# Expert weights in two more slots used once, the residual added in the last pass, selection in two halves

## The reference

```python
x = layer_norm(DN_ALPHA * x + mix, ln1_g[l], ln1_b[l])
ffn = expert_choice_ffn(x, w_router[l], w_gate_up[l], w_down[l])
x = layer_norm(DN_ALPHA * x + ffn, ln2_g[l], ln2_b[l])

def expert_choice_ffn(x, w_router, w_gate_up, w_down):
    aff = jax.nn.softmax(logits, axis=-1)             # 16 experts
    gate, idx = lax.top_k(jnp.swapaxes(aff, 1, 2), cap)   # cap = 64 tokens an expert
    h = jnp.einsum('becd,edf->becf', xs, w_gate_up)   # 1024 -> 2048
    ye = jnp.einsum('becf,efd->becd', jax.nn.silu(hg) * hu, w_down)
    ye = ye * gate[..., None]
    return jnp.zeros_like(x).at[bidx, idx].add(ye)
```

## Time and profile before

| | |
|---|---|
| median of 3 runs | 2457.54 us (2456.19 to 2457.84) |
| the profiled execution | 2456.17 us, its span 2454.4 us |
| TensorE busy / VectorE / ScalarE | 97% / 46% / 35% of the span |
| DMA | 401 MB, mean 163 GB/s |
| granted TensorE clock, mean | 0.990 of full |

### The profile page before, as it was taken

One profiled execution on the slowest core, in us unless ns is written; L12 is line 12 of the kernel. 1 busy time (PEld: TensorE's weight loads), 2 busy tenths in 40 slices (PEclk: granted clock), 3 DMA queues, 4 the chain that ended last, 5 costly groups with the idle time before them and its releaser, 6 DMA issues.

```text
span 2454.4 us, 31324 instructions
## 1 busy us (share of the span) xinstructions
PE 2373.1 (97%) x13306; PEld 1760.8 (72%) x13306; DVE 1137.8 (46%) x1595; ACT 869.1 (35%) x1403; POOL 124.3 (5%) x130
## 2 busy tenths in 40 slices
PE   8999999999999999999999999998999979999997
PEld 6788878888887888888888888865788733443332
DVE  6857676354543324354344463668433552131113
ACT  7554544243433323243233343347322411111111
POOL 0303021100000000000000001200000000000000
PEclk9999999999999999999999999999999989999998
DMA  5121313232224333242222332321322589999996
GB/s 168 70 73 67 104 54 111 70 121 87 102 86 155 120 108 136 79 158 79 93 103 103 112 138 103 115 105 48 127 96 78 200 346 416 429 427 430 428 429 260
DMA packets 117386, 400.97 MB, mean 163 GB/s; under 512 B 6656, under 2 KB 24704, under 8 KB 104320
## 3 DMA queue, kind: packets, MB, share of 16 engines
q1 hardware_dynamic: 113088, 384.29, 40.7%
q0 software_dynamic: 4160, 14.68, 1.7%
HBM read 385.06 MB, written 13.89 MB: 163 GB/s over the span
## 4 chain that ended last, share of the span: by engine, by line
PE 83%; DVE 7%; DMA 6%; ACT 3%; issue 1%; SPq 0%; POOL 0%; DVEq 0%; ACTq 0%; POOLq 0%
PE banks L94 20%; PE banks L96 19%; PE banks L95 19%; PE banks L2251 7%; PE banks L2289 5%; DMA activations_T<-w_gate_up_in 1%; DMA ring<-w_gate_up_in 1%; DMA work<-w_gate_up_in 1%; DVE ring_split L88 1%; DMA work<-o_b 1%; PE banks L1653 1%; DMA ring<-w_up_in 1%; PE banks L1665 1%; PE banks L2030 1%; PE banks L1683 1%
## 5 line engine op out<-in xcount | busy, mean ns | idle before, releaser
L94 PE MATMUL banks<-work_split,ring_split 128*128 128x512 f32 (+1 forms) x1560 | 617.4, 396 | 2.4 <-issue 0.8
L88 DVE TENSOR_TENSOR ring_split<-ring,halves_split 128x1024 fp32r<-128x1024 f32 x281 | 353.5, 1268 | 523.3 <-ACT halves_split L83 522.9
L95 PE MATMUL banks<-work_split,halves_split 128*128 128x512 f32 x1512 | 588.8, 389 | 0.0
L96 PE MATMUL banks<-activations_T_split,halves_split 128*128 128x512 f32 x1160 | 452.3, 390 | 0.0
L83 ACT ACTIVATE halves_split<-ring 128x1024 fp32r<-128x1024 f32 x281 | 293.7, 1055 | 310.9 <-PE banks L96 236.5
L94 PEld LDWEIGHTS banks<-work_split,ring_split 128*128 128x128 f32 x1560 | 293.0, 188 | 70.1 <-issue 8.1
L95 PEld LDWEIGHTS banks<-work_split,halves_split 128*128 128x128 f32 x1512 | 284.1, 188 | 55.7 <-issue 0.5
L96 PE MATMUL banks<-ring_split,work_split 128*128 128x512 f32 (+1 forms) x704 | 270.8, 385 | 0.0
L95 PE MATMUL banks<-halves_split,work_split 128*128 128x512 f32 x672 | 261.6, 389 | 0.0
L96 PEld LDWEIGHTS banks<-activations_T_split,halves_split 128*128 128x128 f32 x1160 | 217.7, 188 | 46.2
L2251 PE MATMUL banks<-work 128*64 128x512 f32 x464 | 150.7, 607 | 4.9 <-DMA work<-w_gate_up_in 2.6
(11 more groups left out here) (387 smaller groups left out, 3166.6 us busy)
## 6 DMA issues: line engine op xcount, KB each, us to landing
ring<-w_in_in SPq DMA_DIRECT2D x30, 2048.0 KB, 7.7
work<-w_gate_up_in SPq DMA_DIRECT2D x29, 2048.0 KB, 26.8
ring<-w_gate_up_in SPq DMA_DIRECT2D x21, 2048.0 KB, 26.2
ring<-w_down_in SPq DMA_DIRECT2D x19, 2048.0 KB, 9.2
work<-w_down_in SPq DMA_DIRECT2D x11, 2048.0 KB, 27.0
ring<-w_in_in SPq DMA_DIRECT2D x17, 1024.0 KB, 7.7
ring<-w_up_in SPq DMA_DIRECT2D x8, 2048.0 KB, 7.9
activations_T<-w_gate_up_in SPq DMA_DIRECT2D x8, 2048.0 KB, 26.9
```

Of the source, the lines that this page charges most:

```text
L88: s.mark(dve.tensor_tensor(R(dst), src, R(hi).bitcast(F32), ALU.subtract), what)
L94: pe.matmul(out, R(ll), R(rh), start=start, stop=False)
L95: pe.matmul(out, R(lh), R(rh), start=False, stop=False)
L96: return pe.matmul(out, R(lh), R(rl), start=False, stop=stop)
```

## The change

- **Slots.** `XH` (until it is filled with rows) takes load 0, and `acc` takes load 10; both are used once as slots. `slot_no` and `former` give the slot of a load and the load that was in it before; the other nine rotate over the rest. From load 20 on, load c again follows load c - 9.
- **Order of loads.** Loads 0 to 3 at first, 4 to 7 and 10 after `m31`, 8 after the logits, 9 after `x31`. Loads 11 to 19 come in halves, each half after half of the group that it follows. Load 11 follows load 1, 12 and 13 follow 2 and 3, and so on.
- **XH.** ScalarE writes `XH` block 0 only after group 0.0.
- **Residual.** `acc` is written by a copy in pass 0. In pass 6 VectorE re-adds high and low part in `XR` (`whole`), SP then broadcasts gain and bias into `XH`, between loads 90 and 91, and in pass 7 `keep` adds the residual to `acc`, a block at a time; `kept(n, t)` waits for block t.
- **Selection.** The 512 tokens of each expert stand as two rows of 256, on partitions 0 to 15 and 32 to 47. Both rows' 64 best are found together; the 64th best of the union is a threshold, and comparisons with it, summed over tokens by matmuls, give the places, equal values behind larger ones.

```diff
--- before.py
+++ after.py
...
-        lnrow = acc[:, 2:4, :]
...
+        posN = cols[:, 32:96].rearrange("p (t e) -> p t e", t=NT)
...
+        lnrow, kept_tmp = XH[:, 0:2, :], XH[:, 2:4, :]
...
-        eslot = [slot5, slot6, ring[2], ring[0], ring[1], ring[3], slot4, AT, slot8]
-        ES = len(eslot)
-        lnrow2 = eslot[(12 * NE // 2 - 8) % ES].rearrange("p k n -> p (k n)")[:, 0:2 * DM].rearrange("p (a b) -> p a b", a=2)
+        once = [x.rearrange("p t d -> p (t d)").rearrange("p (k n) -> p k n", k=KB) for x in (XH, acc)]
+        eslot = [slot5, slot6, ring[2], ring[0], ring[1], ring[3], slot4, AT, slot8] + once
+        ES = len(eslot) - 2
+
+        def slot_no(c):
+            return ES if c == 0 else ES + 1 if c == ES + 1 else (c - 1 if c <= ES else c - ES - 2) % ES
+
+        def former(c):
+            return c - ES - 1 if c <= 2 * ES + 1 else c - ES
+
+        lnrow2 = eslot[slot_no(12 * NE // 2 - 8)].rearrange("p k n -> p (k n)")[:, 0:2 * DM].rearrange("p (a b) -> p a b", a=2)
...
+            def flat(c):
+                return eslot[slot_no(c)].rearrange("p k n -> p (k n)")
+
             def load_half(sem, c, h, what):
...
+                part = slice(h * 2048, h * 2048 + 2048)
+                sem.mark(sp.dma_start(flat(c)[:, part], expert_rows(c // 12, c % 12)[:, part]), what)
+
+            def load(c):
+                e_w[slot_no(c)].mark(sp.dma_start(flat(c), expert_rows(c // 12, c % 12)), f"w{c}")
+
+            def freed(c):
+                return former(c) % 12 // 2, former(c) // 12
+
+            for c in range(4):
+                load(c)
+            sp.wait_ge(*l_pe("m31"))
+            for c in range(4, 8):
+                load(c)
+            load(ES + 1)
+            sp.wait_ge(*q_pe("logits"))
+            load(8)
+            sp.wait_ge(*l_act("x31"))
+            load(ES)
+            c = ES + 2
+            while former(c) < 10:
+                cs = [n for n in (c, c + 1) if freed(n) == freed(c)]
+                for h in range(2):
+                    sp.wait_ge(*e_pe(("half", "group")[h] + f"{freed(c)[0]}.0"))
+                    for n in cs:
+                        load_half(e_w[slot_no(n)], n, h, f"h{n}" if h == 0 else f"w{n}")
+                c += len(cs)
+            for c in range(c, LAST + 1):
+                n, p = freed(c if c < LAST else c + 1)
+                if (n, p) == (5, NE // 2 - 2) and freed(c - 1) != (n, p):
+                    sp.wait_ge(*e_vec("whole3"))
+                    for n, name in enumerate(("ln1_g_2", "ln1_b_2")):
+                        l_row.mark(sp.dma_start(lnrow[:, n, :], T[name].broadcast_to([P, DM])), name)
+                    n, p = freed(c)
+                sp.wait_ge(*e_pe(f"group{n}.{p}"))
+                if c < LAST:
+                    load(c)
                 else:
...
                     for h in range(2):
                         for e in range(2):
-                            load_half((e_h if h == 0 else e_w)[e if h == 0 else (c + e) % ES], c + e, h, f"{'hw'[h]}{c + e}")
+                            load_half((e_h if h == 0 else e_w)[e if h == 0 else slot_no(c + e)], c + e, h, f"{'hw'[h]}{c + e}")
...
-            for q in range(4):
+            first_T(0)
+            for q in range(1, 4):
                 first_T(q)
+                if q == 1:
+                    act.wait_ge(*e_pe("group0.0"))
+                    high(act, e_act, XH[:, 0, :], XR[:, 0, :], "XH0")
                 high(act, e_act, XH[:, q, :], XR[:, q, :], f"XH{q}")
...
             pe.wait_ge(*q_vec("aff"))
-            for t in range(NT):
-                mm = pe.transpose(psum[3][0:NE, t * P:(t + 1) * P], affN[:, t, :], ident)
+            for u in range(2):
+                mm = pe.transpose(psum[3][0:HB, u * P:(u + 1) * P], wide[:, u * HB:(u + 1) * HB], ident)
             q_pe.mark(mm, "affT")
-            pe.wait_ge(*q_vec("pos"))
-            for t in range(NT):
-                mm = pe.transpose(psum[2][:, t * NE:(t + 1) * NE], cum[0:NE, t * P:(t + 1) * P], ident[0:NE, 0:NE])
-            q_pe.mark(mm, "posN")
+            pe.wait_ge(*q_vec("thr"))
+            q_pe.mark(pe.transpose(psum[2][:, 0:NE], thr_row[0:NE, 0, :], ident[0:NE, 0:NE]), "thr")
+            pe.wait_ge(*q_vec("marks"))
+            pe.matmul(psum[1][:, 0:2 * NT * NE], m_incl, marks.rearrange("p a t e -> p (a t e)"), start=True, stop=False)
+            at = psum[1][:, 0:2 * NT * NE].rearrange("p (a t e) -> p a t e", a=2, t=NT)
+            for t in range(NT - 1):
+                pe.matmul(at[:, :, t + 1:, :], ones, marks[:, :, t:t + 1, :].broadcast_to([P, 2, NT - 1 - t, NE]), start=False, stop=False)
+            pe.wait_ge(*q_vec("above"))
+            q_pe.mark(pe.matmul(at[:, 1, :, :], thr_row[0:NE, 1, :], ident[0:NE, 0:NE].unsqueeze(1).broadcast_to([NE, NT, NE]), start=False, stop=True), "posN")
...
             def kept(n, t):
-                pe.wait_ge(*e_vec(f"acc{4 * n + t}.{NE // 2 - 2}"))
+                pe.wait_ge(*e_vec(f"kept{t}"))
                 pe.matmul(psum[final_banks[4 * n + t]][:, :], ident, acc[:, t, n * 512:(n + 1) * 512], start=True, stop=False)
...
-                    if p == 0 and q == 0:
-                        e_pe.mark(mm, "half0.0")
+                    if p == 0:
+                        e_pe.mark(mm, f"half{q}.0")
                     e_pe.mark(rows(q, 1), f"group{q}.{p}")
...
+                    if p == 0 and k == 1:
+                        e_pe.mark(mm, "half4.0")
...
             dve.wait_ge(*q_pe("affT"))
             for r in range(EC // 8):
-                left = wrk[0:NE, :] if r else psum[3][0:NE, :]
-                q_vec.link(dve, dve.max(m8[0:NE, :], left))
-                q_vec.link(dve, dve.match_replace(wrk[0:NE, :], m8[0:NE, :], left, -1.0))
-            q_vec.link(dve, dve.tensor_scalar(wrk[0:NE, :], wrk[0:NE, :], 0.0, None, ALU.is_lt))
-
-            q_vec.link(dve, dve.tensor_tensor_scan(cum[0:NE, :], affT[0:NE, :], wrk[0:NE, :], 0.0, ALU.mult, ALU.add))
-            q_vec.mark(dve.tensor_tensor(cum[0:NE, :], cum[0:NE, :], wrk[0:NE, :], ALU.mult), "pos")
+                left = wrk[0:48, :] if r else psum[3][0:48, 0:256]
+                m8 = best[0:48, 8 * r:8 * r + 8]
+                q_vec.link(dve, dve.max(m8, left))
+                if r < EC // 8 - 1:
+                    q_vec.link(dve, dve.match_replace(wrk[0:48, :], m8, left, -1.0))
+            a, b = best[0:NE, :], other[0:NE, :]
+            q_vec.link(dve, dve.tensor_copy(b, best[32:48, :]))
+            q_vec.link(dve, dve.tensor_tensor(a, a, b[:, ::-1], ALU.max))
+            q_vec.link(dve, dve.tensor_reduce(lmax[0:NE, 0:1], a, AX, ALU.min))
+            q_vec.mark(dve.tensor_copy(thr_row[0:NE, 0, :], lmax[0:NE, 0:1].broadcast_to([NE, P])), "thr")
+            dve.wait_ge(*q_pe("thr"))
+            thr = psum[2][:, 0:NE].unsqueeze(1).broadcast_to([P, NT, NE])
+            dve.tensor_tensor(marks[:, 0, :, :], affN, thr, ALU.is_gt)
+            q_vec.mark(dve.tensor_tensor(marks[:, 1, :, :], affN, thr, ALU.is_equal), "marks")
+            q_vec.link(dve, dve.tensor_tensor(a, a, lmax[0:NE, 0:1].broadcast_to([NE, EC]), ALU.is_gt))
+            q_vec.link(dve, dve.tensor_reduce(lsum[0:NE, 0:1], a, AX, ALU.add))
+            q_vec.mark(dve.tensor_copy(thr_row[0:NE, 1, :], lsum[0:NE, 0:1].broadcast_to([NE, P])), "above")
             dve.wait_ge(*q_pe("posN"))
             dve.wait_ge(*q_ld("wr"))
-            q_vec.link(dve, dve.tensor_copy(posN, psum[2][:, 0:NT * NE].rearrange("p (t e) -> p t e", t=NT)))
+            q_vec.link(dve, dve.tensor_tensor(places, marks, psum[1][:, 0:2 * NT * NE].rearrange("p (a t e) -> p a t e", a=2, t=NT), ALU.mult))
+            q_vec.link(dve, dve.tensor_tensor(posN, places[:, 0, :, :], places[:, 1, :, :], ALU.add))
...
                 if not last:
                     choose(p + 1)
+                else:
+                    keep()
...
+                if p == NE // 2 - 2:
+                    for t in range(NT):
+                        e_vec.mark(dve.tensor_tensor(XR[:, t, :], R(XR[:, t, :]).bitcast(F32), R(XH[:, t, :]).bitcast(F32), ALU.add), f"whole{t}")
...
-                        if p:
+                        if p == 0:
+                            e_vec.mark(dve.tensor_copy(a, psum[scatter_banks[m]][:, :]), f"acc{m}.{p}")
+                        else:
                             dve.wait_ge(*e_vec(f"acc{m}.{p - 1}"))
-                        e_vec.mark(dve.tensor_tensor(a, psum[scatter_banks[m]][:, :], a, ALU.add), f"acc{m}.{p}")
+                            e_vec.mark(dve.tensor_tensor(a, psum[scatter_banks[m]][:, :], a, ALU.add), f"acc{m}.{p}")
                     if m == 0:
...
+
+            def keep():
+                dve.wait_ge(*l_row("ln1_b_2"))
+                for t in range(NT):
+                    tmp = kept_tmp[:, t % 2, :]
+                    turned = lambda x: x.rearrange("p (q j) -> p q j", j=KB)
```

(36 more changed lines are left out.)

15 lines of the change are left out of this document (10 added, 5 removed).

## The result

| | median of 17 | lowest to highest | profiled execution |
|---|---|---|---|
| before | 2456.70 us | 2454.70 to 2457.94 | 2456.17, span 2454.4, clock 0.990 |
| after | 2461.05 us | 2458.83 to 2464.23 | 2460.71, span 2458.9, clock 0.991 |

Ratio 1.0018, 95% interval 1.0012 to 1.0025: 4.4 us slower. The interval leaves out 1, so the changed kernel is slower, by a little less than the 0.2% that the prediction took for the smallest difference it could tell. Forecast: 2460.8, which is 3.3 above the median known then; within 2453 to 2465.

The account below looks back on a forecast made before the run. Bound by the weight-load stream from load 21, issued when group 0.1 ends, to load 89, then by TensorE. Selection -4.8, residual +6.5 and clock +1.65 give +3.3 on the median 2457.54: 2460.8 us, range 2453 to 2465.

Parts of the forecast that it names:

- Stream of loads: Expert stage: DMA unbroken from load 21, issued about 2048.9 at group 0.1's end after 5 us empty, to load 89.
- Slots and halves worth 0: Before group 0.1 ends: two more early loads and halved loads 11 to 19 gain 0, since load 21 still waits.
- The rival of the slots that pay: Around 2048: load 21 freed earlier lets the stream run on, gaining about 6 us; time 2454.8, chance 8%.
- Selection, -4.8: Before group 0.0: shorter rounds save 4.8, later steps 0.5 worse, first transposes 0.5 better; -4.8 us, bounds 3.5 and 6.5.
- The rival of a selection that gains little: Selection: rounds of 1.2 us and more hops, so only -2.5; sum +5.6, time 2463.1, chance 5%.
- Residual, +6.5: Last pass: group 3.7 waits for the second residual block, starting 17.1 us after load 89 instead of 10.6; +6.5 us.
- The rival of a hidden sum: Last pass: broadcasts land early or kept matmuls don't wait, so only the selection counts; -4.8, time 2452.7, chance 10%.
- the one of a broadcast 2 us later than its bytes: Last pass: broadcasts land 2 us late, with both clock spells; sum +6.7, time 2464.2, chance 17%.
- Clock, +1.65: Last pass: TensorE's stops before the two kept matmuls lower its granted clock; +1.65 us, bounds 0 and 3.
- before's slow group 2.7: Last pass of before: after a 2.66 us stop at low clock, group 2.7 took 8.70 us instead of 7.04.
- Sum: Whole kernel: -4.8 + 6.5 + 1.65 = +3.3 us, added to the median 2457.54 gives 2460.8.
- the dip that before had: At 2054 in before, traffic falls to 229 GB/s for 2 us; at most about 1 us could be gained there.

Follow-up runs that it names:

- xh_slot: Changed kernel without the slot in acc, which starts with the residual in pass 0 as before; XH still takes load 0, halves stay: 2452.20 us, 0.9985 of before.
- sel_only: Kernel before with only the selection in two halves; slots, loads and residual as before: 2452.01 us, 0.9983 of before.
- whole_reuses: Changed kernel with loads 11 to 19 issued whole instead of in halves: 2461.36 us, 1.0020 of before.
- old_selection: Changed kernel with the selection of before (one row of 512 tokens an expert, prefix sum): 2464.24 us, 1.0034 of before.
- rows_first: Changed kernel with the gain and bias broadcasts issued ahead of load 89 instead of load 91: 2454.77 us, 0.9996 of before.
- rows_later: Changed kernel with the gain and bias broadcasts one load later, between loads 91 and 92: 2465.75 us, 1.0038 of before.
- kept_warm: Changed kernel with seven unused matmuls more in pass 7, four before the first kept matmul, three before the second: 2459.80 us, 1.0012 of before.
- sel_halves: sel_only with loads 21 and 22 in halves tied to the halves of group 0.1: 2453.64 us, 0.9985 of before.
- xh_quarters: xh_slot with loads 21 and 22 in quarters, each issued when that quarter of group 0.1 is done: 2451.87 us, 0.9980 of before.
- rows_quarters: rows_first with loads 21 and 22 in quarters, each issued when that quarter of group 0.1 is done: 2453.57 us, 0.9988 of before.

## Why the prediction was right

**Stream of loads.** Right, though on an anchored time. Load 21 was due at 2048.9 and came at 2050.15; 0.9 of these 1.25 us is the common part's later arrival. DMA had been empty for more than 5 us by then, as forecast. Group 0.1 started 3.6 us earlier than in before (2043.09 against 2046.66), or 4.5 earlier from the anchor.

**Slots and halves worth 0.** Right: `xh_slot` equals `sel_only`, `whole_reuses` equals the changed kernel, and the idle window stood where it was forecast. The rival of the slots that pay fell with it. The quarters show that the gap was a real reserve, though only about half of its 7.3 us was won back: the Trainium skill, "Perfetto Trace Analysis", section DMA Optimizations, holds that splitting may finish the whole sooner when DMA engines are generally idle. In halves ahead of the gap it gave nothing here, in quarters across the gap 1.5 and 3.1 us in the profiles (0.5 and 1.4 in the medians, which do not show it by themselves).

**Selection, -4.8.** Measured -4.2. The step that was mis-sized is "then 448 columns on TensorE at 0.26 us per 128, 0.9, with hops ... 1.25 in all". It took 2.6: a float32 matmul is two instructions where the row that I priced it by, a transpose, is one, and five narrow matmuls cost 1.0 us more than their columns. The 448 were miscounted too, there are 384, which hid a little of it. So the part behind the rounds grew by 1.5 us, not 0.5 (4.85 against 3.34). The rounds gave 4.7 (11.94 against 7.24), the first transposes 0.6, and the gather 0.4 that I had not counted (5.08 against 5.49): -4.7 - 0.6 + 1.5 - 0.4 = -4.2. That 0.4 is not the selection's: in the eleven profiled executions with the new selection the gather took 4.50 to 5.49 us, by when the clock came up, and in `old_selection` 4.84. So the step itself is worth 3.8, and the size of the whole was hit better than its terms. A round was 0.97, forecast 0.95; by the Trainium skill, "VectorE: DVE Perf Modes", section on the fixed latency, whose rule for a float32 addition of N elements is (N + 151)/0.96 ns, the estimate for 256 elements is 0.424 us, and the trace has 0.42 for MAX8 and 0.40 for the replace. The rival of a selection that gains little (rounds of 1.2, -2.5) fell.

**Residual, +6.5.** Right to 0.1 in its mechanism: landing 7.4 us behind load 89, blocks of 4.35, second block ready at 16.25 against 16.2, then a kept matmul. `rows_first` and `rows_later` moved the landing to either side and the time went with it, -5.8 and +5.0 us, so it is this wait and not the four blocks' own work. The rival of a hidden sum fell; the one of a broadcast 2 us later than its bytes fell too, it landed on its bytes.

**Clock, +1.65.** The mechanism was right, the size is 2.0: 1.1 in the second kept matmul (2.07 against 0.95) and 0.9 in group 3.7 (7.93 against 7.04). `kept_warm` removed 1.8 of it in the profile; the medians differ by 1.3. I had expected before's slow group 2.7 to stay; it ran at full speed in the profiled execution (7.09) and that gained nothing, since the next wait is for the broadcasts.

**Sum.** In the anchored profile it is -4.2 for the selection, -0.3 for groups 0.0 to 5.0, -0.5 from the issue of load 21 to load 89 (342.4 us against 342.9, about the dip that before had, of which I had said that at most 1 us could be gained) and +8.6 in the last pass (6.6 and 2.0): 3.6, where 3.3 was forecast. The errors of the terms, 0.6 too much gain and 0.4 too little loss, were partly made good by those 0.8. The medians differ by 4.4; the 0.8 beyond the anchored 3.6 lie within what an interval leaves open. The common part, which the anchor takes out, was 0.9 later in this one pair of executions, but that it is so in the median is not shown. That 2460.8 and 2461.05 lie 0.25 apart is partly luck: the median of before came out 0.8 lower than the one that the forecast started from, and the loss about 1 us higher.

## What to carry to other kernels

A buffer lent out as a load slot moves its own first use later; price that use at the new place, with the queue in front of it, before you count the load. Here two slots gave nothing, since the stream was bound by when an old slot came free, and the rent of one of them was 8 us; the same small transfer two loads earlier in a full queue cost only 2.8. Price a matmul by a row of a matmul of its type and width, with its weight loads, and never by a transpose.

## What the runs showed of the hardware that was not expected

- The part that all kernels share ended at 1951.5 to 1954.9 us in the thirteen profiled executions. That is as much as this change is worth, so profiles must be compared from an anchor.
- The length of a stop did not by itself tell whether the clock fell. Before group 2.7, stops of 2.66 us (before), 2.65 (`xh_slot`), 2.37 (`sel_halves`) and 2.40 (`xh_quarters`) were followed by seven or eight slow matmuls (most 1.06 us instead of 0.59), in `xh_quarters` only behind four fast ones, and the group took 8.6 to 8.8 us. Stops of 2.40 to 2.72 in the five kernels whose last pass waits for the late residual, and of 3.03 in `sel_only`, went with full speed and 7.1. That is 1.6 us. With one profiled execution of each kernel it is not shown whether this is chance or belongs to the kernel.
- Seven idle matmuls in two waits kept the clock at full speed and saved 1.8 us in the profile.
- Where the stream restarts from an empty queue, loads in quarters of 0.5 MB moved 188 to 410 GB/s, microsecond by microsecond, from 2047 to 2054 (`rows_quarters`). In `xh_quarters`, where the queue did not run empty, the same pieces moved 389 to 418 from 2051 to 2056; whole loads behind a full queue hold 429.
